# A two-sequence decoder layer in split float32: feed-forwards in two token halves, the up projection by Strassen's product

## What is computed

```
ada = silu(c) @ w_ada + b_ada                       # 9 vectors of 1024 for each sequence
h = modulate(rms_norm(x, ln1), sh1, sc1)
g, u = jnp.split(h @ w_up, 2, axis=-1)              # 1024 -> 2 x 2816
x = x + 0.5 * g1 * ((silu(g) * u) @ w_down)         # 2816 -> 1024
...                                                 # mixing stage, then the same with ln2, w_f2_up, w_f2_down
y = rms_norm(x, ln_final)
```

## Time and profile before

| | |
|---|---|
| median of 3 runs | 2152.92 us (2151.82 to 2154.35) |
| profiled execution | 2158.94 us, its span 2157.2 us |
| PE busy | 2081.7 us, 97% of the span |
| PEld, DVE, ACT, POOL busy | 92%, 48%, 26%, 6% |
| mean granted TensorE clock | 0.976 |
| moved by DMA | 160.15 MB, 74 GB/s on average |

### The profile page before, as it was taken

The page is one execution under the profiler, slowest core; times in us unless marked ns, Lnnn a source line. Parts: engine busy times, 40 slices in busy tenths (PEclk is TensorE's granted clock), DMA queues, the critical chain, the costliest instruction groups (busy, mean ns, idle before and its releaser), DMA issues.

```text
span 2157.2 us, 31934 instructions
## 1 busy us (share of the span) xinstructions
PE 2081.7 (97%) x12627; PEld 1978.7 (92%) x12627; DVE 1030.4 (48%) x2060; ACT 551.5 (26%) x893; POOL 120.7 (6%) x139
## 2 busy tenths in 40 slices
PE   6899999999999999989999898999999999999997
PEld 3699999999999999978898888999999999999996
DVE  4753343344244334347666776544424443344336
ACT  2512111111111211245545553411121112111213
POOL 3100000000000000110303311100000000000000
PEclk7899999999999999999999998999999999999998
DMA  9323212212212321133343334111111111111102
GB/s 351 119 63 90 67 49 88 78 39 78 78 53 63 97 59 49 50 98 98 98 108 98 108 89 115 57 39 59 39 40 40 56 39 49 47 40 39 58 1 83
DMA packets 204050, 160.15 MB, mean 74 GB/s; under 512 B 5378, under 2 KB 177273, under 8 KB 203977
## 3 DMA queue, kind: packets, MB, share of 16 engines
q1 hardware_dynamic: 203821, 159.16, 24.6%
q10 hardware_dynamic: 164, 0.09, 0.0%
HBM read 153.43 MB, written 5.91 MB: 74 GB/s over the span
## 4 chain that ended last, share of the span: by engine, by line
PE 85%; DVE 7%; ACT 3%; issue 2%; POOL 1%; DMA 1%; SPq 0%; POOLq 0%; DVEq 0%; ACTq 0%
PE bank L380 79%; PE bank L386 2%; DVE tmp L1066 1%; DVE mwl L1051 1%; POOL tmp L996 1%; DMA ai<-in_w_ada 1%; DVE hl L1086 1%; PE bank L395 1%; DVE yst L1203 1%; DMA ws<-in_w_ffn_up 0%; DVE xT L1113 0%; ACT mwh L741 0%; PE bank L610 0%; PE bank L605 0%; ACT wh L741 0%
## 5 line engine op out<-in xcount | busy, mean ns | idle before, releaser
L380 PE MATMUL bank<-hh,wh 128*128 128x384 f32 (+1 forms) x2112 | 697.6, 330 | 3.5 <-DVE tmp L1140 1.7
L380 PE MATMUL bank<-hl,wh 128*128 128x384 f32 (+1 forms) x2112 | 692.0, 328 | 0.0
L380 PE MATMUL bank<-hh,wl 128*128 128x384 f32 (+1 forms) x2112 | 691.5, 327 | 0.0
L380 PEld LDWEIGHTS bank<-hh,wh 128*128 128x128 f32 x2112 | 397.4, 188 | 40.4 <-issue 36.0
L1140 DVE TENSOR_TENSOR tmp<-tmp,bank 128x384 f32<-128x384 f32 x132 | 70.2, 532 | 735.2 <-ACT tmp L785 735.2
L380 PEld LDWEIGHTS bank<-hl,wh 128*128 128x128 f32 x2112 | 397.5, 188 | 0.4 <-issue 0.2
L380 PEld LDWEIGHTS bank<-hh,wl 128*128 128x128 f32 x2112 | 397.4, 188 | 0.0
L785 ACT ACTIVATE tmp<-bank 128x384 f32<-128x384 f32 x132 | 62.4, 473 | 1201.7 <-PE bank L380 1201.6
L1113 DVE SCALAR_TENSOR_TENSOR xT<-bank,ada,xT 128x384 f32<-128x384 f32 (+1 forms) x552 | 310.9, 571 | 101.8 <-PE bank L380 99.3
L380 PE MATMUL bank<-ah,wh 128*128 128x384 f32 (+1 forms) x1056 | 346.4, 328 | 4.4 <-DVE al L1142 2.3
L380 PE MATMUL bank<-al,wh 128*128 128x384 f32 (+1 forms) x1056 | 344.4, 326 | 0.0
(11 more groups left out here) (172 smaller groups left out, 1500.3 us busy)
## 6 DMA issues: line engine op xcount, KB each, us to landing
ws<-in_w_ffn_up SPq DMA_DIRECT2D x88, 512.0 KB, 4.7
ws<-in_w_in SPq DMA_DIRECT2D x51, 512.0 KB, 3.9
ws<-in_w_ffn_down SPq DMA_DIRECT2D x44, 512.0 KB, 4.3
aws<-in_w_ada SPq DMA_DIRECT2D x88, 256.0 KB, 2.8
ai<-in_w_ada SPq DMA_DIRECT2D x7, 2048.0 KB, 18.2
ws<-in_w_out SPq DMA_DIRECT2D x24, 512.0 KB, 3.8
out_y_p<-yst SPq DMA_DIRECT2D x8, 512.0 KB, 2.6
xin<-in_x_prompt SPq DMA_DIRECT2D x3, 512.0 KB, 6.3
```

The costliest lines, as they stand in the source:

```text
L380: mm = pe.matmul(out, l(k), r(k), start=(k == 0 and a == 0), stop=(k == depth - 1 and a == 2))
```

## The change

Both feed-forwards are run once over tokens 0 to 543 and then once over tokens 544 to 1087 (`HALF` = 544), each time over all 11 blocks, so every feed-forward weight is loaded, split and used twice. A "round" below is one block for one half of the tokens; there are 44. A round has two "visits", f = 0 and f = 1, one for each tile of 128 gate and 128 up columns.

In a visit the four products (gate, up) x (first 272, last 272 tokens of the half), each of two depth halves of 512, are eight half-depth products of 128 x 512 by 512 x 272. They are now seven, by Winograd's form of Strassen's product: sums and differences of the four weight quarters (`st`, made by POOL) and of the four activation quarters (made once for each half, by POOL, and kept in `xo` in both parts) are multiplied, and the outputs are put together from the seven banks with copies and sums (ACT `snapshot` into `pp`, POOL `combine_products`, DVE `combine`). Each of the seven weight operands of 128 x 512 is split for itself (`woh`, `wol`; `w_high`, `w_low`). The down projection of a round is made inside the first visit of the next round, between products 3 and 4; its outputs are pairs of banks, added to `xT` by one DVE instruction of 544 or 480 columns (`residual`).

```diff
@@ sizes @@
-LATE = (0, 3, 6, KT)
+HB = 272
+HALF = 2 * HB
+NPR = 7
+WSLOT = (0, 1, 2, 3, 0, 1, 2)
+BANK = ((0, 1, 2, 3, 4, 5, 0), (1, 2, 3, 4, 5, 1, 2))
@@ PE @@
+            def up(blk, f, j, new, after_mix):
+                until(pe, s_wlo, blk, 2 * NPR, NPR * f + j + 1)
...
+                out = ps[BANK[f][j]][:, 0:HB]
+                s = WSLOT[j]
+                for k in range(4):
+                    for a, (w, x) in enumerate(((woh, 0), (woh, 1), (wol, 0))):
+                        mm = pe.matmul(out, w[:, s, P * k:P * (k + 1)], x_operand(j, x)[:, k, :],
+                                       start=(k == 0 and a == 0), stop=(k == 3 and a == 2))
+                mm.then_inc(s_m, 1)
@@ ACT, one visit @@
+                    for j in (2, 3):
+                        w_high(blk, f, j)
...
+                    snapshot(blk, f, 0)
+                    if not (c == 0 and at == 0 and f == 0):
+                        a_high(blk, f)
+                    for j in (4, 5):
+                        w_high(blk, f, j)
...
+                    w_high(blk, f, 6)
...
+                    snapshot(blk, f, 1)
+                    silu(blk, f, 0)
+                    snapshot(blk, f, 2)
...
+                    if f == 0:
+                        wd_high(blk, 0)
+                        wd_high(blk, 1)
+                    if not (c == 1 and at == NB - 1 and f == 1):
+                        w_high(*next_visit(blk, f), 0)
+                        w_high(*next_visit(blk, f), 1)
...
+                    silu(blk, f, 1)
@@ POOL, one visit @@
+                    combine_g(blk, f)
...
+                    combine_products(blk, f)
...
+                    if not (c == 1 and at == NB - 1 and f == 1):
+                        combine_su(*next_visit(blk, f))
@@ DVE, one visit @@
+                    for j in (2, 3):
+                        w_low(blk, f, j)
...
+                        act_products(blk, f)
...
+                    combine(blk, f, 0)
+                    for j in (4, 5):
+                        w_low(blk, f, j)
...
+                        if j == 4:
+                            combine(blk, f, 1)
...
+                    w_low(blk, f, 6)
...
+                            residual((blk[0], blk[1] - 1), 0 if c == 0 or at == 0 else 1, m, gain, (b, NB * which - 1))
...
+                        wd_low(blk, 0)
+                        wd_low(blk, 1)
...
+                    combine(blk, f, 2)
+                    last = c == 1 and at == NB - 1 and f == 1
+                    if not last:
+                        w_low(*next_visit(blk, f), 0)
+                    combine(blk, f, 3)
+                    if not last:
+                        w_low(*next_visit(blk, f), 1)
```

More of the change, by code:

```diff
@@ L29 @@
 F = 2816
-NF = F // P
 FB = 2
-NB = NF // FB
+NB = F // (FB * P)
 CH0 = (0, 384, 768)
@@ L123, in __call__, with until, every_block @@
         self.eng.wait_ge(self.sem, self.n if self.base is None else self.base + self.n)
+def until(eng, sem, blk, per, plus):
+    b, base = blk
+    if isinstance(b, int):
+        if per * (b + base) + plus > 0:
+            eng.wait_ge(sem, per * (b + base) + plus)
+    else:
+        eng.wait_ge(sem, b * per + (per * base + plus))
+def every_block(eng, which, block):
+    for c in range(2):
+        for seg in SEGMENTS[which, c]:
+            if isinstance(seg, int):
+                block(which, c, seg, None)
+            else:
+                with eng.Fori(seg[0], seg[1]) as b:
+                    block(which, c, b, seg[2])
 def program(nc, i, o):
@@ new lines, in down @@
+            def down(blk, half):
+                until(pe, s_al, blk, FB, FB)
+                until(pe, s_wdlo, blk, FB, FB)
+                for m in range(KT):
+                    until(pe, s_xacc, blk, KT, m - 1)
+                    for t in range(2):
+                        n0, n = ((HB * t, HB) if half == 0 else (H1W * t, H1W + NS * t))
+                        out = down_pair(m, 0, n)[:, t, :]
+                        for k in range(FB):
+                            for a, (w, x) in enumerate(((wdh, ah), (wdh, al), (wdl, ah))):
+                                mm = pe.matmul(out, w[:, k, P * m:P * (m + 1)], x[:, k, n0:n0 + n],
+                                               start=(k == 0 and a == 0), stop=(k == FB - 1 and a == 2))
+                    mm.then_inc(s_down, 1)
@@ L992, in norm @@
+            def norm(q):
+                n = NCOL[q][1]
+                gp.wait_ge(n_ss, q)
+                for k in range(KT):
+                    gp.wait_ge(n_sq, KT * (q - Q_MIX) + k + 1)
                     if k == 0:
@@ new lines, in half_scale, with norm @@
+            def half_scale(half, part, k0, k1):
+                q = (0, 2, 7, 9)[half] + part
+                c0, n = NCOL[q]
+                for k in range(k0, k1):
+                    dve.scalar_tensor_tensor(out=y_tile(half, KT * part + k), in0=xT[:, k, c0:c0 + n], scalar=coef[:, 2 * (half // 2), k, 0:1],
+                                             in1=norm_tile(q, "R")[:, 0:n], op0=ALU.mult, op1=ALU.mult).then_inc(y_k, 1)
+            def norm(q, part):
+                if part == 0:
+                    norm_factor(q)
+                    return
+                if q >= Q_F2:
+                    if part >= 2:
+                        half_scale(2, q - Q_F2, part - 2, part - 1)
+                    return
+                c = q - Q_MIX
@@ L1119, in add_residual, with residual @@
                 ins.then_inc(done, 1)
-            def ada_sums(bank):
-                dve.tensor_copy(aev[:, :], bank[:, :]).then_inc(s_aevc, 1)
+            def residual(blk, half, m, gain, samples):
+                if m == 0:
+                    until(dve, s_xacc, blk, KT, 0)
+                until(dve, s_down, blk, KT, m + 1)
+                n0, n = (0, HB) if half == 0 else (HALF, H1W)
+                xs = xT[:, m, n0:n0 + 2 * n].rearrange("p (a n) -> p a n", a=2)
+                ins = dve.scalar_tensor_tensor(out=xs, in0=down_pair(m, 0, n), scalar=ada[:, gain + m, 0:1], in1=xs, op0=ALU.mult, op1=ALU.add)
+                if half:
+                    t = rt[:, m % 2, :]
+                    dve.tensor_tensor(seqs(t), seqs(down_pair(m, n, NS)[:, 1, :]),
+                                      ada[:, gain + m, 1:9].unsqueeze(2).broadcast_to([P, NSEQ, TSEQ]), ALU.mult).then_inc(s_rs, 1)
+                    until(dve, s_rs, samples, KT, m + 1)
+                    ins = dve.tensor_tensor(xT[:, m, SEQ:TOK], xT[:, m, SEQ:TOK], t, ALU.add)
+                ins.then_inc(s_xacc, 1)
@@ L1478, in _ @@
             dve.wait_ge(m_x, KT * NC)
-            ffn_all(1, W_F2, 8 * KT, False)
-            for t in range(3, 9):
+            every_block(dve, 1, ffn)
+            act_products((0, 4 * NB), 0)
+            final(3)
+            for m in range(KT):
+                residual((0, 4 * NB - 1), 1, m, 8 * KT, (NB - 1, NB))
+            for t in range(4, 9):
                 final(t)
```

1268 lines of the change are left out of this document (770 added, 498 removed).

## The result

The changed kernel takes **2604.2 us** (median of 4 runs, 2600.3 to 2606.4) beside 2153.6 us for the kernel before on the same chip: a ratio of 1.209 [1.206, 1.211]. The forecast was 2371 us with a range up to 2450. The direction was right and the size was not: 450 us more than before where 218 were expected. The experiments look for the other 230.

What follows compares the result with a forecast made beforehand. PE's matmuls bound the kernel before; after, DVE's chain with POOL's holds makes rounds 41.3 us. Feed-forwards +127 and +71, edges +20: 2158.9 + 218 = 2377 profiled, median 6.0 lower, 2371 us; range 2125 to 2450.

Steps and rivals of the forecast that it cites:

- PE's own pace: Matmuls of 272 columns on PE take 126.9 ns each, 33.5 us a round against 35.5 for half an old block.
- Lone prices: DVE and ACT instruction times without collisions: split of 512 columns 695 ns, bank sum 437, residual of 544 780.
- The chain: Hand-overs between engines make PE wait at named places: a round of 41.3 us, 35.7 without POOL's holds.
- The slow clock hidden in visit 1's wait before product 4: Visit 1's first products at half speed lose 1.5 us, most of it inside the wait before product 4.
- The rival of a slow clock: Every wait drops PE's clock, or the 272-column pitch stops at 147 ns: round 43.5 to 44, 2480 us; chance 0.10.
- The turns: Each of two turns to the second half puts seven splits of 1088 (1.29 us each) on DVE: +12 to +15 each.
- The last rival: The change does not thin PE's work; rejected, as the order shows 84 matmuls of 272 columns a visit; no chance given.
- the size of POOL's hold: POOL's adds shut DVE's two-SBUF-input instructions out for 0.84 us at 512 columns, 0.45 at 272; lone add of 512 1.04.
- The prediction's sentence on the Trainium skill's rule: Blocking for the whole instruction, 1.04 us for 0.84, with seven collisions would add 1.2 us a round, 53 us in all.
- The waits by their places: PE late per round: product 2 0.5 us, down 1.1, residuals 0.65 [1.0], end of visit 0 3.4, visit 1's product 4 2.0.
- The conditioning unit: In twelve rounds its pieces lie where PE waits anyway; its copy puts 0.6 us on DVE in visit 1.
- the edges: Turns, last down projections, one conditioning unit fewer and an early norm: together about +20 us, from -10 to +45.

Runs made afterwards that it cites:

- experiment 2: Changed kernel plus 26 unused matmuls of 272 columns filling PE's wait before product 0 of visit 1 in 34 loop rounds; 2649.4 us, 1.228.
- experiment 1: Changed kernel with POOL's weight and product sums touching only 16 columns in the 34 loop rounds; 2399.2 us, 1.112.
- experiment 4: Changed kernel with POOL making visit 1's two weight sums early, in visit 0 ahead of its product sums; 2559.2 us, 1.185.

## Why the prediction was wrong in size

**Held.** *PE's own pace*: three matmuls in 0.38 us is 126.7 ns, 126.9 forecast. *Lone prices*: low part of 512 columns 0.70 (0.695), bank sum 0.43 (0.437), residual 0.78 (0.78). *The chain*: the waits of the prediction stand where it said, but for the one before product 4 of visit 1, and with POOL's sums made short a round is 35.8 where the clock stays up (35.7), the wait at the end of visit 0 is 1.8 (1.9). *The slow clock hidden in visit 1's wait before product 4*: experiment 2. The rival of a slow clock had 43.5 to 44 us for a round, and 43.5 and 43.9 were measured: its number came true by chance, since with the clock kept at 1.00 the round is as long. *The turns*: 15 us each, 12 to 15 forecast, in part by luck: a split took 1.9 us where 1.29 was forecast for it, and short splits freed only 10 of the 15. *The last rival*: PE's work got thinner as the order said.

**The step that failed in the rounds is the size of POOL's hold.** The prediction took 0.84 us for a sum of 512 columns and a lone sum at 1.04, scaled from adds of 384. Alone, such a sum takes 1.26 us here (the shortest of 88), one of 272 columns 0.77, one of 16 columns 0.22 in experiment 1. The products meet it with +0.93 and +1.06 over 0.44, and the run in pieces shows why: the wait is for the whole instruction. By the line through 272 and 512 columns one of 396 would take 1.02 us, but the lone add of 396 in the earlier trace rows took 0.85; why it is shorter is open. The prediction's sentence on the Trainium skill's rule had the whole instruction right and gave +1.2 us a round for it (seven times 0.2 is 1.4), about half of what is missing; the other half is the length of the sum. The Trainium skill ("SBUF — State Buffer", section "Who interferes with whom") calls the ports that VectorE and GpSimd share "an exclusive lock", for which a VectorE instruction with two inputs in SBUF contends with a GpSimd instruction that reads SBUF. This trace agrees by the 0.93 and 1.06 above, and I had let the adds of 384 columns overrule it. For the length of the sum the same holds: the Trainium skill ("GPSIMD Engine Reference", section "3.1 Elementwise — side-by-side cycle accounting") has 2.6 cycles for each element of a sum with two inputs, an estimate of 1.11 us plus a fixed part for 512 columns; the 1.26 measured agrees and my 1.04 does not. The waits by their places, forecast and measured: product 2 0.5 and 1.1, down 1.1 and 1.35, residuals 0.65 and 0.8, end of visit 0 3.4 and 3.9, visit 1's first four products 2.0 and 2.5 (nearly all of it slow clock in the round shown). That is 2.0 us; some 0.1 for each start after a wait makes 2.4, and 44 rounds make 105. The conditioning unit costs 1.3 us in its 12 rounds instead of 0.6: PE waits 3.1 us in each for the weights of pieces 4 to 7 (37.3 us in 12 times), where the prediction had no wait for a transfer.

**The step that failed at the edges is an omission.** The prediction costed the turn's splits and nothing of the norm for the second half that the change lays into blocks 0 and 1: 14 additions, 16 scaling steps and the samples' steps on POOL, ahead of the weight sums in the same queue. Made short they free 55 us. The turn's splits, made short, free 27, but that much was in the forecast (24 to 30), so they are no part of the miss. By stage, from the first matmul of each feed-forward to its last, in the two profiled executions: the feed-forwards are 216 and 249 us longer than before, of which the rounds are 136 and 179, so 79 and 70 stand at their edges, where 33 were forecast. The start is 13 us shorter, the stretch between the feed-forwards and the end are 3 each (13 forecast in all). Of the 116 us too much inside the feed-forwards the norm is 55, and 61 are not settled. They lie in the first two rounds of each first half, still 15 to 18 us above two steady ones with the norm's steps short, in the rounds next to a turn, 3 to 5 us longer than steady ones, and at the first and last products of each feed-forward. GpSimd's combinations at the turn, which the prediction did not price either, are a candidate that no run tests.

## What to carry to other kernels

Before work is moved to a second vector engine, write the two queues side by side and mark every pair that is released by the same event: such a pair collides nearly every time (84 and 86 of 88 times here), for one whole instruction, and the one on the critical path should be let through first (one wait here: 98 us). Work that is moved to an engine with much slack still stands in its queue: ask what is queued behind it in the first and last block too, where preparation of the next stage sits. And when a price has to be carried to another size, take it from two sizes, or give the Trainium skill's number more weight than one scaled row.

## What the runs showed of the hardware

A wait of 3.9 us was followed by 4.9 us of matmuls at 227 ns instead of 126 in one round, by 13 to 24 such matmuls in the others of that half, with a round of 43.5 to 43.7 us in all but the last before the turn; with the wait filled with matmuls the clock stayed at 1.00 in the round shown, and it was worth nothing, since DVE's chain ended last. In the kernel with short sums a wait of 1.83 us was followed by 14 to 16 slow matmuls in some rounds and by none in others, and there they cost 1.1 us a round. An instruction of VectorE with both inputs in SBUF and one of GpSimd exclude each other for a whole instruction: cutting GpSimd's in four cut VectorE's wait from 1.07 to 0.26 us, at the same number of elements. What reads one input from PSUM was not held: in the changed kernel 133 of the 264 bank sums into `pp` ran beside a POOL sum and took 0.43 us like the others, and in experiment 4 residuals of 544 columns took 0.77 us beside one and 0.78 alone.
